# Moving the split of the next FFN's first weight pair behind six of the eight residual columns at each mixer's end

## What is computed

```
h = h + 0.5 * swiglu(norm(h), w1, w3, w2)      stages 0, 2, 3, 5, 6, 8, 9, 11
h = h + mixer(norm(h))                         stages 1 (ab), 4 (cd), 7 (hy), 10 (sw)
swiglu(h) = (silu(h @ w1) * (h @ w3)) @ w2     w1, w3: 1024 x 2752, w2: 2752 x 1024
norm(x) = x * rsqrt(mean(x*x) + eps) * g       (stages 0 to 5: then * (1 + scale) + shift)
```

## Time and profile before

| | |
|---|---|
| median of 3 executions | 1736.59 us (1734.52 to 1738.09) |
| the profiled execution, its own time | 1735.33 us |
| its span, first to last instruction | 1733.5 us |
| mean granted TensorE clock, share of full speed | 0.928 |
| TensorE matmuls busy | 1484.0 us, 86% |
| VectorE busy | 1386.3 us, 80% |
| ScalarE busy | 988.7 us, 57% |
| DMA | 420.30 MB, mean 242 GB/s |

### The profile page before, as it was taken

The page is one execution under the profiler, slowest core; times in us unless marked ns, Lnnn a source line. Parts: engine busy times, 40 slices in busy tenths (PEclk is TensorE's granted clock), DMA queues, the critical chain, the costliest instruction groups (busy, mean ns, idle before and its releaser), DMA issues.

```text
span 1733.5 us, 27728 instructions
## 1 busy us (share of the span) xinstructions
PE 1484.0 (86%) x11160; PEld 1411.6 (81%) x11160; DVE 1386.3 (80%) x2275; ACT 988.7 (57%) x1643; POOL 9.6 (1%) x24
## 2 busy tenths in 40 slices
PE   4987775868886988889699999899899999987997
PEld 4977765767776877687599899897799999876997
DVE  7587765788888888886878888887588888876886
ACT  4444453564446444653666766656566676766765
POOL 0000000000000000000000000000000000000000
PEclk9698988989998989899899999998899999999999
DMA  8499955458984899442589677543587677633783
GB/s 342 181 343 334 353 190 199 154 214 290 328 328 174 324 350 349 168 158 93 207 302 339 245 263 281 203 154 110 212 277 277 232 268 278 242 111 147 270 281 128
DMA packets 84972, 420.30 MB, mean 242 GB/s; under 512 B 9363, under 2 KB 9795, under 8 KB 58094
## 3 DMA queue, kind: packets, MB, share of 16 engines
q1 hardware_dynamic: 82910, 410.59, 65.6%
q0 software_dynamic: 1936, 7.95, 1.3%
HBM read 417.37 MB, written 1.13 MB: 241 GB/s over the span
## 4 chain that ended last, share of the span: by engine, by line
PE 50%; DVE 26%; DMA 14%; ACT 7%; issue 2%; SPq 1%; DVEq 0%
PE pw L631 15%; PE pw L632 15%; DMA land_p<-stream 11%; PE acc L631 8%; DVE low_p L1966 8%; PE acc L632 8%; DVE modw L1799 4%; DVE low_d L1966 3%; ACT hi_p L1451 2%; DMA biasT<-wmod 2%; DMA land_d<-stream 1%; DVE proj L1946 1%; PE acc L941 1%; DVE biasT L1799 1%; ACT hi_d L1451 1%
## 5 line engine op out<-in xcount | busy, mean ns | idle before, releaser
L631 PE MATMUL pw<-h_hi,hi_p 128*128 128x256 f32 x2928 | 745.9, 293 | 62.8 <-DVE low_p L1966 45.4
L632 PE MATMUL pw<-h_lo,low_p 128*128 128x256 f32 x2928 | 734.4, 289 | 0.0
L631 PEld LDWEIGHTS pw<-h_hi,hi_p 128*128 128x128 f32 x2928 | 581.1, 198 | 82.2 <-issue 45.5
L1966 DVE SCALAR_TENSOR_TENSOR low_p<-hi_p,land_p 128x1024 fp32r<-128x1024 f32 x418 | 507.3, 1221 | 101.5 <-ACT hi_p L1451 101.2
L632 PEld LDWEIGHTS pw<-h_lo,low_p 128*128 128x128 f32 x2928 | 580.8, 198 | 0.5 <-issue 0.2
L1451 ACT ACTIVATE hi_p<-land_p 128x1024 fp32r<-128x1024 f32 x418 | 434.6, 1049 | 155.0 <-DMA land_p<-stream 154.8
L631 PE MATMUL acc<-a_hi,hi_d 128*128 128x256 f32 x1376 | 366.6, 300 | 76.7 <-DVE low_d L1966 76.2
L632 PE MATMUL acc<-a_lo,low_d 128*128 128x256 f32 x1376 | 362.0, 297 | 0.0
L631 PEld LDWEIGHTS acc<-a_hi,hi_d 128*128 128x128 f32 x1376 | 283.4, 206 | 85.1 <-issue 85.1
L1451 ACT ACTIVATE hi_d<-land_d 128x1024 fp32r<-128x1024 f32 x209 | 219.0, 1048 | 144.0 <-DMA land_d<-stream 144.0
L632 PEld LDWEIGHTS acc<-a_lo,low_d 128*128 128x128 f32 x1376 | 284.0, 206 | 0.0
(11 more groups left out here) (354 smaller groups left out, 1712.4 us busy)
## 6 DMA issues: line engine op xcount, KB each, us to landing
land_p<-stream SPq DMA_DIRECT2D x207, 1024.0 KB, 5.1
land_d<-stream SPq DMA_DIRECT2D x209, 512.0 KB, 5.6
modw<-wmod SPq DMA_DIRECT2D x124, 512.0 KB, 5.4
biasT<-wmod SPq DMA_DIRECT2D x20, 512.0 KB, 6.1
biasT<-bias_rows POOLq DMA_DIRECT2D x3, 1536.0 KB, 11.3
biasT<-bias_rows POOLq DMA_DIRECT2D x1, 3072.0 KB, 12.9
land_p<-stream SPq DMA_DIRECT2D x4, 512.0 KB, 6.6
cst_s<-cst SPq DMA_DIRECT2D x1, 1792.0 KB, 8.9
```

Of the source, the lines that this page charges most:

```text
L631: mm(o, lhs[0], rhs[0], start=start, stop=False, skip_group_check=True)
L632: return mm(o, lhs[1], rhs[1], start=False, stop=stop, skip_group_check=True)
L1966: v.scalar_tensor_tensor(fine[rows], hi[rows], -ONCE, land_block(t, b)[rows], ALU.mult, ALU.add).then_inc(lo_ready, 1)
```

## The change

ScalarE: the two coarse splits of LEAVE leave the end of the mixer functions and come inside the norm of the FFN that follows, after the coarse input and the squares of columns 0 to 5 and before those of columns 6 and 7. VectorE: the two fine splits leave the mixers' ends and come inside residual, after columns 0 to 5 (and the fine inputs of columns 0 to 3 that go with them) and before the wait for triple_used and columns 6 and 7. The order SPLITS, the loads, the slots and TensorE's instructions stay as they are. For FFNs that follow an FFN, LEAVE.get gives an empty list.

```diff
@@ ScalarE, norm_deferred and norm_raw (both the same)
                     if k % 2:
                         for q in (k - 1, k):
                             fn(sq[:, q, :], x[:, q, :], ACT.Square).then_inc(sq_ready, 1)
+                    if k == KD - 3:
+                        split_high(LEAVE.get(n - 1, []))
                 split_high(ENTRY[n])
@@ ScalarE, mixer_sw, mixer_ab, mixer_cd, mixer_hy, last line of each
-                split_high(LEAVE[i])
@@ VectorE, residual
                     if k % 2 == 0 and k < KD - 2:
                         dve.wait_ge(acc_done, 3 * i + k // 2 + 1)
                     elif k == KD - 2:
+                        split_low(LEAVE.get(i, []))
                         dve.wait_ge(triple_used, AFTER[i])
@@ VectorE, mixer_sw, mixer_cd, mixer_hy, mixer_ab, last line of each
-                split_low(LEAVE[i])
```

## The result

The changed kernel takes 1721.55 us (median of 4, 1720.63 to 1724.15) beside 1736.51 us for the kernel before (4 executions): ratio 0.9917, interval 0.9900 to 0.9934. That is 15.0 us less by the medians, 11.5 to 17.4 by the interval; the forecast was 13.5. The profiled execution took 1721.89 us against 1735.33, 13.4 less, and its span is 1720.1 us. Measured twice more beside other kernels, the ratio was 0.9914 (0.9894 to 0.9935) and 0.9924 (0.9905 to 0.9943). One slow execution of the changed kernel (1868.86 us, granted clock 0.72 instead of 0.93) is left out of its ratio and its median. The gain is 13 to 15 us, and the executions of one kernel scatter by several us, so that the terms of 2 to 4 us are read from the traces, and the times only confirm their sums.

A forecast was written before the change was run, and what follows sets the result against it. No single engine bounds the whole run; at four mixer ends, work queues behind a late pair. Terms 1.9 + 3.6 + 4.0 + 4.0 = 13.5 us off 1735.33 give 1721.8, 1723.1 as median; range 1719 to 1727.

The forecast's parts named there:

- ab: End of mixer ab: split starts 1.9 us later, yet the summing of squares comes at 352.75 against 354.73; term 1.9 us.
- cd: End of mixer cd: ENTRY's fine split of pair f+1 at 835.76 instead of 839.38; term 3.6 us.
- hy: End of mixer hy: summing of squares at about 1241.0 instead of 1245.07; term 4.0 us.
- sw: End of mixer sw: same form and distances as at hy; term 4.0 us.
- the next thing late: At cd's end: pair f+1 lands at 834.67, so ScalarE waits for it from 831.9, about 2.8 us.
- TensorE is just not the bound at ab: At ab's end: TensorE starts at 350.35, finishes its first product by 356.4, when ENTRY's first split would be ready.
- The clock: TensorE's clock after the change, which could not be read: taken as zero, with 1.5 us either way kept.
- the winning side: At hy: the second 1.2 GHz stretch on the path (1248.6 to 1252.7) vanishes, another 1.5 us won.
- The losing side: At sw: TensorE gets a 1.2 GHz stretch like hy's second one, 1.5 us lost.
- Rival 3: Slower: TensorE might stay at 1.2 GHz through j = 1, 2 and the first down product; 1745 us; chance 0.03.
- Rival 1: Terms partly swallowed: TensorE or DMA-held FFN at ab, late f+2 loads at hy and sw; 1729 us; chance 0.15.
- late loads of pair f+2 at hy and sw: At the ends of hy and sw: pair f+2 could land too late, with 0.3 us to spare.

The follow-up runs named there:

- the early pair: Kernel before, with POOL's two bias loads (3 MB) held back until the fourth triple of the FFN after cd: ratio 0.9995 (0.9982 to 1.0008).
- the idle products: Changed kernel plus 14 constant products on TensorE between a mixer's last product and the next FFN's first: ratio 0.9926; with early sums of squares too, 0.9884.

## Why the prediction was right

**The terms.** Each was worked out from the columns' work against the landings, and each came out. Summing or ENTRY earlier, forecast and measured: ab 1.9 and 2.17, cd 3.6 and 3.48, hy 4.0 and 3.99, sw 4.0 and 3.84; the sum 13.5 and 13.48. What the stretches to the end of the next FFN show is more, 16.7 us: ab's 1.9 was too small a term, 3.7 by its stretch (why it grows in its FFN is open; the scatter is about 1 us of it), and hy's 5.1 holds the clock, below. So the sum of 13.5 met the time a little by luck: in the two profiled executions the four stretches together are 15.4 us shorter, and the rest of the kernel, which the change does not touch, is 2.0 us longer. The steps hold one by one: the split starts 0.25 us later at hy (forecast 0.1), at 346.61 at ab (346.85), and at cd the next thing late is pair f+1, for which ScalarE waits 2.81 us (2.8). TensorE is just not the bound at ab, as worked out, though with more to spare: its first product starts on the pair's first block, at 349.05 instead of the 350.35 forecast, ends at 355.25, and then it waits for ENTRY's first fine part:

```profile
356.01 0.36 PE L631 MATMUL pw<-raw_both,hi_p 128*128 128x258 f32 x1 [0.77 <-DVE low_p L1966]
```

**The mechanism.** That both engines' queues stood behind the pair is shown by the kernel with VectorE's half alone (no gain), by those with four and eight columns (a longer way to the root), and at cd by the early pair (3.2 us with the old order).

**The clock** was left at zero with 1.5 us on either side, and the winning side came. These are TensorE's stretches at hy in the changed kernel, against the earlier trace rows:

```profile
1232.60:1239.20 6.60, 5.68 (x32) 5.31 (x32) 6.52 (x11) 4.68 (x8) 0.00 (x0) 0.74 0.72 298
1239.20:1242.50 3.30, 2.82 (x22) 2.77 (x23) 3.30 (x4) 1.76 (x3) 0.00 (x0) 1.00 0.72 206
```

The first product is still partly at 1.2 GHz, but j = 1 is at full level, where before it had 0.60. So the root at hy came 5.4 us earlier, not 4.0. The losing side, a slow stretch at sw, did not come in this execution (the root stands 3.92 us behind ENTRY before and after), but in a weaker form in one of the other two: there TensorE's first product ran at a granted clock of 0.50 for 4.3 us, had not ended when ENTRY's first fine part was ready, and the root came 0.6 us later. In the execution shown, the stage of sw gave most of hy's surplus back in another place. From the residual of the FFN ahead to the issue of sw's pair f, before and after (columns as above):

```profile
1508.86:1577.64 68.78, 60.44 (x472) 51.81 (x471) 52.15 (x161) 46.45 (x136) 0.00 (x0) 0.95 0.24 85
```

```profile
1498.72:1568.77 70.05, 61.88 (x472) 52.74 (x472) 52.19 (x161) 47.75 (x137) 0.00 (x0) 0.92 0.24 83
```

It is 1.3 us longer with the same 472 matmuls, at a granted clock of 0.92 instead of 0.95. That the two nearly cancel is chance: over all kernels run here this stretch, which none of them changes, scatters from 68.8 to 70.1 us. The clock alone does not order these lengths (69.3 us at 0.96 in another execution of the changed kernel), so the cause of the scatter is open.

**What I had wrong or loose.** Rival 3 feared slow stretches on the path through waits of 2 to 4 us. In the changed kernel it did not happen in j = 1, but it happened with the idle products at hy: the mechanism is real, and costs 1.5 us at one end, a tenth of what would turn the sign. Rival 1 named ab's term as the one that could be lost, in TensorE's narrow margin or in the FFN behind; neither took it. It also feared late loads of pair f+2 at hy and sw. At sw the prediction took hy's distances over, but f+2 is issued 4.8 us after f there, not 5.8, and landed 9.0 us later instead of 7.6; ScalarE waited for it:

```profile
1582.58 2.01 ACT L1455 ACTIVATE hi_p<-land_p 128x1024 fp32r<-128x1024 f32 x2 [1.02 <-DMA land_p<-stream]
```

It cost nothing, since VectorE's four fine splits of ENTRY still ran without a gap. Among the expectations the weakest was VectorE's half alone: 4 us forecast at most, none found, for the table load left out.

## What to carry to other kernels

Where several engines take their work in written order and one item waits for a late transfer, list what stands behind it and does not need it, and move that in front on every engine at once: VectorE's queue alone gained nothing. Move as much as fits into the wait and no more: the limit is where the item's own consumer (here TensorE's first product) becomes late. And ask for each transfer that is made earlier what it takes from the others: the 3 MB moved out of cd's end brought new waits in the next stage, and the gain was gone at its end.

## What the runs showed of the hardware that I had not expected

TensorE's granted clock fell after short waits. In the changed kernel at hy it idled 2.79 us and then 0.57 us, and the next matmuls were at 1.2 GHz (0.42 us each instead of 0.28). TensorE in order of time:

```profile
1232.90 0.36 PE L631 MATMUL pw<-h_hi,hi_p 128*128 128x256 f32 x1 [2.79 <-DVE low_p L1966]
...
1233.94 0.58 PE L631 MATMUL pw<-h_hi,hi_p 128*128 128x256 f32 x1 [0.57 <-DVE low_p L1966]
1234.32 0.42 PE L632 MATMUL pw<-h_lo,low_p 128*128 128x256 f32 x1
```

With the idle products it fell in the middle of a product after a wait of 1.88 us at hy (0.59 over the 4.0 us behind it), and in the same execution it stayed up after a wait of 1.88 us at sw (1.00 over 4.0 us). At sw before, it stayed up after a wait of 2.85 us (the stretch behind that wait is the earlier trace rows). The Trainium skill, page "TensorE: Matmul & The Clock Gate", section "HAM oscillation — how this bites in real kernels", describes a kernel whose waits for data put each next burst of products at half rate; the trace agrees that a wait can cost the burst behind it, and shows that a wait as long or longer need not: it goes either way.

At cd's end a 1 MB pair needed 4.9 to 5.0 us to land without the 3 MB of POOL's queue beside it, and 8.2 to 11.1 us with them, over all kernels run here.
